# Every third low part of the weights in three projections: from VectorE to ScalarE and an accumulating DMA

## The reference, cut to what matters

```python
def even_mixer(u, w_in, conv_w, a_log, dt_bias, onorm_w, w_out):
    proj = u @ w_in                      # 2048 x 7184: ev_gdn, ev_sb, ev_z below
    ...
    return mixed @ w_out
def second_block(x, p, norm_gain, w_in, ...):
    hn = rmsnorm(h, norm_gain[i])
    proj = hn @ w_in[i]                  # 2048 x 4096: s_in below
    pool_in = proj[..., :POOL_WIDTH]
    ...
```

## Time and profile before

| | us |
|---|---|
| median of 3 runs | 2842.73 |
| lowest and highest | 2835.78, 2842.78 |
| span of the profiled execution, first to last instruction | 2833.9 |
| TensorE matmul busy | 2813.9 |
| TensorE weight load busy | 2332.1 |
| VectorE busy | 2029.3 |
| ScalarE busy | 1471.8 |
| GpSimd busy | 25.2 |

### The profile page before, as it was taken

How to read it: one execution, slowest core, us unless ns; L and a number is a source line. 1 busy time by engine, 2 the same in 40 slices (tenths; PEclk the granted TensorE clock), 3 DMA queues, 4 the chain that set the end, 5 groups by cost and what they waited for, 6 DMA issues and landing times.

```text
span 2833.9 us, 38622 instructions
## 1 busy us (share of the span) xinstructions
PE 2813.9 (99%) x14909; PEld 2332.1 (82%) x14909; DVE 2029.3 (72%) x2719; ACT 1471.8 (52%) x1915; POOL 25.2 (1%) x43
## 2 busy tenths in 40 slices
PE   9999999999999999999999999999999999999998
PEld 8888888888888888888888888888888887888887
DVE  5786865688878887564545588888888667876555
ACT  5554465655545554455455465555555546455444
POOL 0000000000000000000000000000000100000000
PEclk9999999999999999999999999999999999999999
DMA  7543346565655656555554556656665754444553
GB/s 246 178 149 120 120 149 208 178 207 201 220 203 196 216 200 231 194 189 183 168 174 151 191 186 207 215 194 207 207 205 201 251 190 146 149 155 164 197 178 134
DMA packets 256219, 528.28 MB, mean 186 GB/s; under 512 B 9536, under 2 KB 10016, under 8 KB 255056
## 3 DMA queue, kind: packets, MB, share of 16 engines
q1 hardware_dynamic: 250096, 501.61, 52.4%
q0 software_dynamic: 2816, 13.20, 1.4%
q10 hardware_dynamic: 3168, 11.54, 1.0%
HBM read 511.63 MB, written 2.10 MB: 181 GB/s over the span
## 4 chain that ended last, share of the span: by engine, by line
PE 97%; DVE 1%; ACT 1%; issue 0%; DMA 0%; DVEq 0%; ACTq 0%
PE acc L645 67%; PE acc L696 12%; PE side L1113 2%; PE side L1116 2%; PE side L1112 2%; PE acc L1112 1%; PE acc L1116 1%; PE acc L1113 1%; PE side L965 1%; PE acc L752 1%; PE side L798 1%; PE side L958 1%; PE side L850 1%; PE side L1104 0%; ACT ar L1557 0%
## 5 line engine op out<-in xcount | busy, mean ns | idle before, releaser
L2418 DVE TENSOR_TENSOR wlo<-raw,whi 128x1024 fp32r<-128x1024 f32 x532 | 644.8, 1223 | 444.2 <-ACT whi L1568 442.4
L1568 ACT ACTIVATE whi<-raw 128x1024 fp32r<-128x1024 f32 x532 | 557.0, 1059 | 486.3 <-PE acc L645 473.0
L645 PE MATMUL acc<-whi,xh 128*128 128x512 f32 x2152 | 593.2, 397 | 0.2 <-issue 0.2
L1971 ACT ACTIVATE whi<-raw 128x1024 fp32r<-128x1024 f32 x360 | 379.9, 1061 | 402.1 <-PE acc L696 142.0
L645 PE MATMUL acc<-wlo,xh 128*128 128x512 f32 x2152 | 576.8, 390 | 0.2
L645 PE MATMUL acc<-whi,xl 128*128 128x512 f32 x2152 | 576.3, 390 | 0.0
L2928 DVE TENSOR_TENSOR wlo<-raw,whi 128x1024 fp32r<-128x1024 f32 x360 | 438.1, 1222 | 100.9 <-ACT whi L1971 93.0
L645 PEld LDWEIGHTS acc<-wlo,xh 128*128 128x128 f32 x2152 | 403.4, 188 | 86.9 <-DVE wlo L2418 2.2
L645 PEld LDWEIGHTS acc<-whi,xl 128*128 128x128 f32 x2152 | 404.0, 188 | 86.2
L645 PEld LDWEIGHTS acc<-whi,xh 128*128 128x128 f32 x2152 | 394.2, 188 | 78.1 <-issue 0.6
L645 PE MATMUL acc<-whi,hTh 128*128 128x512 f32 x672 | 182.0, 393 | 0.0
(11 more groups left out here) (395 smaller groups left out, 2848.1 us busy)
## 6 DMA issues: line engine op xcount, KB each, us to landing
raw<-in_ffn_w_down SPq DMA_DIRECT2D x88, 1024.0 KB, 5.0
raw<-in_ffn_w_gate SPq DMA_DIRECT2D x68, 1024.0 KB, 5.0
raw<-in_ffn_w_up SPq DMA_DIRECT2D x68, 1024.0 KB, 5.0
raw<-in_ev_w_in SPq DMA_DIRECT2D x56, 1024.0 KB, 5.0
raw<-in_od_w_in SPq DMA_DIRECT2D x48, 1024.0 KB, 5.0
raw<-in_w_in SPq DMA_DIRECT2D x32, 1024.0 KB, 5.2
raw<-in_ffn_w_gate SPq DMA_DIRECT2D x40, 512.0 KB, 3.7
raw<-in_ffn_w_up SPq DMA_DIRECT2D x40, 512.0 KB, 4.5
```

The lines of the kernel that those rows point to most:

```text
L645: mm = pe.matmul(acc[2 * pair + t][:], x[:, k0 + j, t * P:t * P + P], w[:, ring, j], start=start and j == 0, stop=stop and j == 1)
L1568: act.activation(whi[:, place % RING], raw_granule(place), ACT.Copy).then_inc(S("hi_done"), 1)
L1971: act.activation(o, src, ACT.Copy).then_inc(S("hi_done"), 1)
L2418: dve.tensor_tensor(wlo[:, place % RING], raw_granule(place), whi[:, place % RING].bitcast(F32), ALU.subtract).then_inc(S("lo_done"), 1)
```

## The change

In 40 granules (three of each of the last three chunks of ev_gdn, every third of ev_sb from its third on, and every third of s_in from its fifth on except four) VectorE does not make the low part. Instead ScalarE, right after the hi copy, writes the negated copy of the same raw granule, rounded to fp32r, into `wlo`, and GpSimd issues a DMA that adds `raw` to `wlo` in place (SBUF to SBUF, 512 KB). The result is raw - hi as before. Two semaphores, `lo_moved0` and `lo_moved1`, tell of its landing; GpSimd issues moved granule n only when n - 2 has landed. TensorE waits for the landing ahead of the `wlo` sweep, and SyncE refills a slot only when the moved low in it has landed too. Counts of `lo_done` are lowered by the granules that VectorE no longer makes (`made`). A few semaphores are merged under other names (`wpool_in` into `bc_in`, `u_turned` into `c_turned`, `ph_done` into `gh_done`), with their counts adapted.

```diff
+MOVED = sorted([gran("ev_gdn", c, j) for c in (3, 4, 5) for j in (0, 3, 6)] + [gran("ev_sb", 0, 0) + j for j in range(2, 47, 3)]
+               + [gran("s_in", 0, 0) + j for j in range(4, 62, 3) if j not in (10, 13, 19, 22)])
+
+def made(g):
+
+    return g - sum(m < g for m in MOVED)
...
+        def lo_ready(eng, g):
+
+            if isinstance(g, int) and g in MOVED:
+                n = MOVED.index(g)
+                eng.wait_ge(S(f"lo_moved{n % 2}"), 16 * (n // 2 + 1))
+            elif isinstance(g, int):
+                eng.wait_ge(S("lo_done"), made(g + 1))
+            else:
+                eng.wait_ge(S("lo_done"), g + (1 - MADE_LATE))
+
         @block.sync
         def _(sp):
+            def slot_free(n):
+
+                sp.wait_ge(S("lo_done"), made(FREE[n]))
+                for m in moved_in_slot(n):
+                    lo_ready(sp, m)
...
+            def move_lows(first, last):
+
+                for g in MOVED:
+                    if first <= g < last:
+                        n = MOVED.index(g)
+                        place = raw_of(g) % (2 * RING)
+                        pool.wait_ge(S("neg_done"), n + 1)
+                        if n >= 2:
+                            lo_ready(pool, MOVED[n - 2])
+                        pool.dma_start(wlo[:, place % RING], raw_granule(place), accum_op=ALU.add)\
+                            .then_inc(S(f"lo_moved{n % 2}"), 16)
+
+            move_lows(0, GRAN0["ev_z"])
...
             for q in range(2):
+                move_lows(GRAN0["s_in"] + 11 * q, GRAN0["s_in"] + 8 * q + 11)
                 pool.wait_ge(S("projected"), 2 * (PROJ0["s_in"] + q) + 2)
...
+            move_lows(GRAN0["s_in"] + 19, GRAN0["s_in"] + 64)
             pool.wait_ge(S("back2"), 4)
...
             def granule(g, ring, pair, lhs_h, lhs_l, k0, first, last, low=None):
-                    pe.wait_ge(S("lo_done"), g + 1)
+                    lo_ready(pe, g)
...
                 act.activation(whi[:, place % RING], raw_granule(place), ACT.Copy).then_inc(S("hi_done"), 1)
+                if g in MOVED:
+                    act.activation(wlo[:, place % RING], raw_granule(place), ACT.Copy, scale=-1.0).then_inc(S("neg_done"), 1)
...
             def split(g, place=None):
 
+                if g in MOVED:
+                    return
                 place = raw_of(g) % (2 * RING) if place is None else place
```

More of the change, by code:

```diff
@@ L182, in gran, with moved_in_slot @@
     return GRAN0[name] + c * (KTS[name] // 2) + j
+MOVED = sorted([gran("ev_gdn", c, j) for c in (3, 4, 5) for j in (0, 3, 6)] + [gran("ev_sb", 0, 0) + j for j in range(2, 47, 3)]
+               + [gran("s_in", 0, 0) + j for j in range(4, 62, 3) if j not in (10, 13, 19, 22)])
+def made(g):
+    return g - sum(m < g for m in MOVED)
+MADE_LATE = sum(m < GRAN0["up0a"] for m in MOVED)
+def moved_in_slot(n):
+    return [m for m in MOVED if raw_of(m) // 2 == n]
 def shape_constants():
@@ L376, in _ @@
                         for m in range(8):
-                            sp.wait_ge(S("lo_done"), i * MIXED + (FREE[n0 + 12 + m] - 2 * MIXED))
+                            sp.wait_ge(S("lo_done"), i * MIXED + (made(FREE[n0 + 12 + m]) - 2 * MIXED))
                             full = S(f"landed{m % RING}")
@@ L1384, in turn_u @@
                 pe.wait_ge(S("x_spread"), e + 1)
-                b = claim(bank, "u_turned", e + 1)
+                b = claim(bank, "c_turned", e + 3)
                 for r in range(8):
@@ L1502, in glu_aside @@
                     if g == 0:
-                        pe.wait_ge(S("wpool_in"), 16)
+                        pe.wait_ge(S("bc_in"), 80)
                     pe.wait_ge(S("pooled"), g + 1)
@@ L2192, in u_out @@
                 act.wait_ge(S("u_ready"), e + 1)
-                run(ug[:, 8 * e:8 * e + 8], bank[:].rearrange("p (r j) -> p r j", r=8), ACT.Copy, "u_turned")
+                run(ug[:, 8 * e:8 * e + 8], bank[:].rearrange("p (r j) -> p r j", r=8), ACT.Copy, "c_turned")
             def t_out(q, k, bank):
@@ L2329, in s_out_aside @@
                         for t in range(TT):
-                            run(hTh[:, k, t * P:t * P + P], side[t][:, k * P:k * P + P], ACT.Copy, "ph_done")
+                            run(hTh[:, k, t * P:t * P + P], side[t][:, k * P:k * P + P], ACT.Copy, "gh_done")
             linear("s_out", lambda c: None, lead, s_out_aside)
@@ L3084, in down_mixed @@
                             dve.wait_ge(S("hi_done"), g + 1)
-                            dve.wait_ge(S("lo_done"), g)
+                            dve.wait_ge(S("lo_done"), made(g))
                             tt(wx, b[:, 1], b[:, 3], ALU.add, "wmix_done")
@@ L3089, in down_mixed @@
                             lo(g, b[:, 0::2])
-                            dve.wait_ge(S("lo_done"), g + 1)
+                            dve.wait_ge(S("lo_done"), made(g + 1))
                             dve.wait_ge(S("wmix_done"), sums + 2)
@@ L3547, in s_out_aside @@
                 if (c, j) == (2, 4):
-                    dve.wait_ge(S("ph_done"), 4)
+                    dve.wait_ge(S("gh_done"), 8)
                     for t in range(TT):
```

20 lines of the change are left out of this document (10 added, 10 removed).

## The result

| | median of runs | range of runs | profiled execution: time, span |
|---|---|---|---|
| before | 2842.49 us (10 runs) | 2835.68 to 2842.78 | 2835.78, 2833.9 us |
| after | 2849.24 us (10 runs) | 2847.88 to 2850.53 | 2848.53, 2846.5 us |

The ratio of the runs is 1.0037 (95% interval 1.0028 to 1.0045): slower, and all ten runs after lie above all ten before. The two medians are only 6.75 us apart, 0.24%. The two profiled spans lie 12.6 us apart, and why that is nearly twice the difference of the medians is the first thing the runs had to explain.

What follows compares the result with a forecast made beforehand. TensorE was taken as the bound. Stalls at tight granules, 4D - 12.45, less 0.55 us recovered, gave 9.0 us at D of 5.5 us; set on the median, 2842.7 + 9.0 = 2851.7 us, range 2841 to 2874.

Steps and rivals of the forecast that it cites:

- What bounds the kernel: TensorE, busy 2813.9 of 2833.9 us; taking 48.9 us of low splits off VectorE was worth only 0.55 us.
- ScalarE's copies at nothing: 40 negated copies of 1.06 us, 42 us on ScalarE, fit its idle time; cost taken as nothing.
- No new wait for `whi`: Sign expected in the profile after: TensorE's matmuls get no new wait for ScalarE's hi copies.
- The budgets: Time from hi copy's start to `wlo` sweep: 4.1 to 6.4 us at granules 30, 32, 38, 46, 908, 911.
- D: Time of the accumulating DMA from GpSimd's issue to landing, estimated at 5.5 us, ends 2.9 and 10.6 us.
- recovered: First chunk of s_in: two `wlo` sweeps late behind VectorE, 0.3 and about 0.24 us, give back 0.55 us.
- the joint term: Granules 908 and 911 in s_in together stall TensorE for D - 2.65 us.
- second stream: The accumulate also reads its destination; one more 512 KB was put at 2.1 us of D.
- contention as a side of the range: Weight loads take about half of the DMA engines' time, favouring D above 5.5 us; the estimate stayed at 5.5.
- Rival (c): VectorE's work holds up GpSimd's descriptors near granule 911: 1 to 2 us once, 2853 to 2854; chance 0.38 shared with forecast.
- nothing takes a stall back later: Since TensorE is the bound, the stalls count in full: 9.0 us at D of 5.5 us.
- the line of 8.5 us or 0.3%: Smallest change a measurement can tell from none; the sum crosses it at D = 5.4 us; slower 0.53, same 0.41.

Runs made afterwards that it cites:

- the split: Kernel before with each of the two blocks of 128 small matmuls in s_in halved around a weight granule; median 2836.43 us, ratio 0.9991.

## Why the prediction was right, and where it was wrong

**What bounds the kernel: right.** TensorE did, and 45 us less on VectorE bought under a microsecond. The run without the DMAs measures it: 0.9 us.

**ScalarE's copies at nothing: right.** "No new wait for `whi`" held in the profile after and in the run without DMAs. The run in which VectorE waited for the copies is no counterexample; its cost came through VectorE's queue.

**The budgets: right, place by place.**

| place | forecast at D of 5.5 us | measured |
|---|---|---|
| 30 and 32 | 3.6 | 1.40 + 2.22 = 3.62 |
| 38 | 1.3 | 1.14 |
| 46 | 1.8 | 1.42 |
| 908 and 911 | 2.85 | 2.79 + 0 |
| recovered | -0.55 | -1.0 |
| sum | 9.0 | 8.0 |

They named the stalled granules, all but one, and that none of the 34 others would stall; moving those alone cost nothing. That 911 had no stall of its own was contained in the joint term. What was recovered was undersized: the prediction took the late starts alone, and the sweeps behind them had been longer too.

**D: the right size from wrong parts.** The estimate was 2.9 (plain copy) + 2.1 (second stream) + 0.5 (issue) = 5.5 us. Measured: 2.9 with the issue inside it, + 1.6 for accumulating (0.3 of it in the longer issue and start), and 0 to 5.8 us behind a weight load. The median of 5.3 and the 5.8 to 6.8 us of the five tight ones lie near 5.5 because the missing term makes up for the two that were too large; that is luck. What decides D at 30, 32, 38 and 46 is the 1 MB load beside the DMA: the landing comes 2.8 us after that load's last packet, and a DMA issued 1 us sooner (30) only waited longer. At 908 it comes 3.8 us after it, most likely for the packet of the instruction queue shown above. The prediction had contention as a side of the range, "weight loads take about half of the DMA engines' time", not as the term it is; therefore I expected the earlier issue to help, and behind a load it didn't. The Trainium skill, DMA: Bandwidth & Descriptors, section "Queues, rings and completion order", has each DMA engine taking turns between its queues; by that the two transfers would share the engines from the start, while here they overlap only for the load's last 0.3 to 1.7 us, in eleven of 13 cases. Whether the engines' order or the descriptors' way keeps the accumulate back isn't settled by any run. Rival (c), descriptors held up by VectorE (the Trainium skill, SBUF — State Buffer, "Who interferes with whom"), left no mark: with VectorE 70% busy, 23 of 40 started within 1.5 us of the issue, and with the load held back the first packets of 30, 32, 38 and 46 came 1.4 to 1.5 us after the issue too.

**The missing step: TensorE's clock.** The prediction said that nothing takes a stall back later; it didn't ask whether a stall costs more than its length. In the profiles half clock began with or within 1.5 us behind stalls of 2.05, 2.08, 2.40, 2.62, 2.77, 2.79, 2.98 and 3.07 us; behind the others, 0.46 to 2.37 us, it did not. Each such stretch costs about 1.6 us where it covers a granule. Two of them, and some 0.5 us of slower matmuls behind the stalls, come on top of the stalls less what was given back (7.4 us with the split, 8.0 without). So the change costs 11.0 us with the split and 12.6 by the profiled spans, 0.9 of these in the first ten microseconds. The Trainium skill, TensorE: Matmul & The Clock Gate, section "HAM oscillation — how this bites in real kernels", warns of idle gaps of TensorE for this reason; the rows bear it out, with gaps shorter than those that it speaks of, and add a case without a gap, the dense blocks of small matmuls. Why some stalls of 2.03 to 2.37 us were followed by it and others not, no run shows.

**The median.** 2851.7 us was forecast and 2849.24 measured, a miss of 2.5 us that comes of two others: the cost on an undisturbed clock was put 2 to 3 us too low, and the median that it was set on contained about 7 us of half clock in s_in, most of which the changed kernel did not have. The two misses have opposite signs, and that the sum came so near is luck. I took the spread of 2835.8 to 2842.8 us of three runs for noise around one value; it was separate groups with a cause, and the profiled execution, at 2833.9, was of the lowest. The chances put slower at 0.53 with the sum on the line of 8.5 us or 0.3%. By the ratio of the runs (1.0037, and 1.0036 with the split) the line is passed narrowly; by the medians, 6.75 us, it isn't.

## What to carry to other kernels

A DMA in a chain of tight deadlines has a landing time that the transfers beside it set: measure its budget from the profile, then ask which load is in flight when it is issued (and whether a packet of the instruction queue falls into it), since an earlier issue gains nothing behind a load and holding the load back moves the stall to the next one. Where the bound engine is TensorE, relieving an engine with 70% of busy time buys only the waits that end with it, here 0.9 us for 49 us of work, and any new wait is at risk of costing its length and a stretch of half clock as well. Look at the granted clock in several executions of the kernel before, before a median is used as the base of a sum.

## What the hardware showed that was not expected

- At the end of a block of 128 back-to-back 64x16 matmuls (3.9 us at full clock), in which TensorE never stands, PEclk falls to 0.5 for 3.4 or 6.8 us in some executions, six of the 18 blocks of nine profiles; 3.2 us are lost per stretch of 6.8 us ((2841.1 - 2833.9 - 0.8 in the opening) / 2). With two halves of 64 and a granule between them it is in none of five profiles, and the eleven spans of the split kernel leave no room for it.
- An accumulating DMA of 512 KB from SBUF to SBUF takes 843 ns to issue on GpSimd and 4.5 us to land, a plain one 528 ns and 2.9 us; both can wait for a 1 MB load that runs ahead of them, up to 10.3 us in all (granule 950, whose low part nobody was waiting for yet).
- A 16 KB packet of the instruction queue among the packets of such a DMA goes with a landing of 5.8 to 6.4 us instead of 4.5 to 5.1, in four of 23 that started promptly.
- Half clock also came from 352 to 355 us, for 3.4 us, in four of the profiles that had stalls before 205 us and in none that had not. What links the two is open.
